# Pattern sums moved to GpSimd and merge weights spread by ScalarE and transposed, in the second layer's new-token attention

## The chip, the cores and the metric
One Trainium2 chip, one NeuronCore of it. The metric is the device time of one launch in microseconds, median of three runs.

## The reference, cut to what matters
The kernel runs one inference step of a two-layer decoder for a prompt of 1024 tokens and for 8 sample sequences of 8 new tokens each. Layer 2 attends with three head groups of different window and dilation over shared keys and values; the group outputs are merged with weights that are their softmax denominators, normalised over the groups.

```python
B_PATTERNS = ((128, 1), (512, 4), (2048, 16))       # (window, dilation), 8 heads of 64 each

def combine_groups(outs, lses):
    wts = jax.nn.softmax(jnp.stack(lses, axis=0), axis=0)
    return jnp.einsum('gnts,gntsd->ntsd', wts.astype(outs[0].dtype), jnp.stack(outs, axis=0))

def dilated_sample(q, kc, vc, slopes):
    S = q.shape[1]
    W = kc.shape[1] - S
    outs, lses = [], []
    for gi, (w, r) in enumerate(B_PATTERNS):
        steps = jnp.arange(w // r + 1)
        idx = W + jnp.arange(S)[:, None] - r * steps[None, :]
        valid = idx >= 0
        idx = jnp.maximum(idx, 0)
        kg = kc[:, idx]
        vg = vc[:, idx]
        s = jnp.einsum('bshd,bskhd->bhsk', q[:, :, gi], kg).astype(jnp.float32) * HEAD_DIM ** -0.5
        s = s - slopes[gi][None, :, None, None] * (r * steps).astype(jnp.float32)
        s = jnp.where(valid[None, None], s, NEG)
        lse = jax.nn.logsumexp(s, axis=-1)
        p = jnp.exp(s - lse[..., None])
        outs.append(jnp.einsum('bhsk,bskhd->bshd', p.astype(vc.dtype), vg))
        lses.append(jnp.swapaxes(lse, 1, 2))
    return combine_groups(outs, lses)
```

## The kernel before, in words
All activations stay in SBUF with features on partitions. The projections (L1447) are the bulk of the span: each weight block is split into a high and a low part, and three fp32r products are made of it. The order of the work is written out by hand: every engine has its own program, and they meet at semaphores that count completed steps.

The change touches one stage. After the attention of the second layer over the prompt (scores L1754, transposes of probabilities L1766, values L1783) come eight batches of new tokens, b = 0 to 7, one per sample sequence. They share one softmax over the three patterns, so the eight heads' rows of a batch hold 1344 columns of `PSB`: 512 for dilation 16, 512 for dilation 4, 128 for dilation 1, and 3 x 64 for the new tokens themselves. Per batch:

- `sample(b)` on GpSimd (L578) stages the queries into `SQN`, two buffers in turn.
- `sample_scores(b)` on TensorE (L1802 to L1811) makes the scores of all patterns; it waits until VectorE has read those of the batch before (`sb_ttr`).
- `sample(b)` on VectorE (L1333, L1339) adds the penalties in four pieces and keeps a running minimum, each piece waiting for the one before; `sample(b)` on ScalarE (L860) exponentiates all 1344 columns in place.
- `sample_turn(b)` on TensorE (L1835) transposes the probabilities by matmuls with the identity. A key that belongs to several patterns gets the sum of its probabilities: the matmuls of its segments accumulate into the same PSUM columns (14 matmuls).
- ScalarE (L868) and VectorE (L1357, L1358) copy the result to `PTS`; `sample_values(b)` on TensorE (L1860, L1862) multiplies with the values.
- ScalarE scales by the reciprocal sum (L875), TensorE transposes the output back (L1867), ScalarE and VectorE write its high and low parts (L882, L1365).

Between these steps stands the merge of the prompt's three pattern outputs, cut into 8 pieces (p, h), where `pieces(b)` gives batch 0 two of them, batches 1 to 6 one each, and batch 7 none. A piece has three rows, g = 0 to 2, numbered n = 3(2p + h) + g. `merge_row` on TensorE (L1823) spreads the weights `CW` of one pattern over 128 features into PSUM, with the weight column broadcast over 64 as the stationary operand and the identity moving (8 matmuls); `merge_product` on VectorE (L1314) multiplies the pattern's output with it; GpSimd (L587) adds the three. Every second batch, ScalarE and VectorE write the merged output's high and low parts (L886, and `merge_lo`, L1318).

TensorE's order in a batch is: scores of b + 1, turn of b, merge rows 0 and 1, values of b, merge row 2, output transpose of b, further rows. ScalarE's is: exponential of b + 1, copy to `PTS` of b, scaling of b, and the output parts. VectorE's: penalties of b + 1, copies to `PTS` of b, products, output parts. GpSimd's: staging of b + 2, adds. ScalarE and VectorE prepare the first weights of the output projection at the end of batch 6.

```python
            for b in range(NEWB):
                if b + 1 < NEWB:
                    sample(b + 1)
                sample_keys(b)
                sample_norm(b)
```

Of the kernel before, what the change touches and what calls it, by code (L numbers as in the profile page):

```python
# [20 lines left out]
P = 128  # L21
DM = 1024
SEQ = 1024
NEWB, NEWT = 8, 8
NEW = NEWB * NEWT
TOK = SEQ + NEW
KT = DM // P
HD = 64
# [3 lines left out]
NG = len(PATTERNS)  # L32
# [16 lines left out]
R16, R4, R1 = 512, 512, 128  # L49
# [43 lines left out]
def program(nc, t):  # L93
    from contextlib import ExitStack
    ctx = ExitStack()
    with ctx:
        base = [16512]

        def at(name, shape, off, dt=F32):
            return nc.alloc_sbuf_tensor_at(name, shape, dt, offset=off)  # L100

        def take(nbytes):
# [7 lines left out]
        o_xh, o_xl = take(KT * W4 + 256), take(KT * W4 + 256)  # L110
# [6 lines left out]
        IDN = at("IDN", [P, P], take(512))  # L117
# [54 lines left out]
        CM = at("CM", [P, 2, 8, 16], R + 71680)  # L172
        CW = at("CW", [P, NG, 8, 8], R + 72704)
        CS = at("CS", [P, NG, 8, 8], R + 73472)
        CT = [at("CT0", [P, 8, 8], R + 74240), at("CT1", [P, 8, 8], R + 74496)]
        TSB = at("TSB", [P, R16 + R4 + R1], R + 74752)

# [6 lines left out]
        PSB = at("PSB", [P, 2, SCOLS], o_xl + 16384)  # L184
        PTS = at("PTS", [P, 7, P], o_xl + 27136)
        PS = ctx.enter_context(nc.psum_tensor("PS", [P, 8, 512], F32))
# [1 line left out]
        names = """raw0 raw1 wh wl slab free0 free1 vps vev_act vev_dve const ones gain pad  # L188
            sq sqs sums std rb eps xh xn xfree silu gt yg yt yout tch tres tsq tadd tcol tstd trst trow scaled hh hx
            qev a_free a_score a_ttr a_exp a_rl a_norm a_tr a_pev0 a_pev1 a_pv a_out ohi olo xre  # L190
            score ttr exp tr pev0 pev1 pv oev stats cm0 cm1 c_d c_x c_op coef c_t c_mul c_add c_hi c_lo
            tabA nsink tab1 tab4 tab16 kperm vnew vst_out vg0 vg1
            cA tsa sa_q sa_s sa_ttr sa_exp sa_es sa_p sa_tr sa_evA sa_evD sa_pv sa_out sa_outlo
            home0 home1 home2 home3 home4 tsb sb_stage sb_zero sb_s sb_ttr sb_exp sb_p sb_tr sb_evA sb_evD sb_pv sb_os sb_otr sb_oh sb_ol
            ka0 ka1 khalf kwh kwl turn rows_out copies""".split()
        S = {n: ctx.enter_context(nc.semaphore("s_" + n)) for n in names}
        xin = [ctx.enter_context(nc.semaphore(f"s_xin{k}")) for k in range(KT)]
# [75 lines left out]
        def pieces(b):  # L273

            return (0, 1) if b == 0 else (b + 1,) if b + 1 < NEWB else ()
# [206 lines left out]
        def _(pool):  # L482
# [89 lines left out]
            def sample(b):  # L572
                if b >= 2:
                    pool.wait_ge(S["sb_s"], b - 1)
                for kk in range(2):
                    src = QB[64 * kk:64 * kk + 64, :].rearrange("p (a g n) -> p g a n", a=4, g=NG)[:, :, :, SEQ + b * NEWT:SEQ + (b + 1) * NEWT]
                    dst = SQN[b % 2][64 * kk:64 * kk + 64, :, :, 8 * kk:8 * kk + 8]
                    nc.gpsimd.tensor_copy(dst, src).then_inc(S["sb_stage"], 1)  # L578

            def add(p, h):  # L580

                n = 2 * p + h
                for g in (1, 2):
                    pool.wait_ge(S["c_mul"], 3 * n + g + 1)
                    if n or g == 2:
                        pool.wait_ge(S["c_add"], 2 * n + g - 1)
                    nc.gpsimd.tensor_tensor(as_tokens(natural(0, p, h).rearrange("p i r -> p (i r)"), g),  # L587
                                            as_tokens(natural(0, p, h).rearrange("p i r -> p (i r)"), g), natural(g, p, h),
                                            ALU.add).then_inc(S["c_add"], 1)
            sample(0)  # L590
            pool.wait_ge(S["sb_stage"], 2)
            pool.wait_ge(S["score"], C2)
            nc.gpsimd.memset(SQN[1][:], 0.0).then_inc(S["sb_zero"], 1)
            pool.wait_ge(S["sb_zero"], 2)
            sample(1)
            for b in range(NEWB):
                if b + 2 < NEWB:
                    sample(b + 2)
                pool.wait_ge(S["sb_stage"], 2 * min(b + 3, NEWB))
                for n in pieces(b):  # L600
                    add(n // 2, n % 2)
                    pool.wait_ge(S["c_add"], 2 * n + 2)
# [5 lines left out]
        def _(act):  # L608
# [237 lines left out]
            for s in range(C3 + T_LAG):  # L846
                n = len(CALLS[s]) if s < C3 else 0
# [15 lines left out]
            def sample_keys(b):  # L863

                act.wait_ge(S["sb_tr"], 2 * b + 1)
                if b:
                    act.wait_ge(S["sb_pv"], b)
                nc.scalar.copy(PTS[:, 0:4, :], PS[:, 5, :].rearrange("p (c n) -> p c n", c=4)).then_inc(S["sb_evA"], 1)  # L868

            def sample_norm(b):  # L870
                act.wait_ge(S["sb_pv"], b + 1)
                act.wait_ge(S["sb_p"], b + 1)
                if b:
                    act.wait_ge(S["sb_otr"], b)
                nc.scalar.activation(OS[:], PS[:, 7, 0:P], ACT.Copy, scale=SM[:, 8 + b % 2:9 + b % 2]).then_inc(S["sb_os"], 1)  # L875

            def sample_out(b):
                act.wait_ge(S["sb_otr"], b + 1)
                for kk in range(2):
                    src = PS[64 * kk:64 * kk + 64, 7, P:2 * P].rearrange("p (a n) -> p a n", a=4)[:, :, 8 * kk:8 * kk + 8]  # L880
                    dst = outputs(QBR, 1)[64 * kk:64 * kk + 64, :, SEQ + b * NEWT:SEQ + (b + 1) * NEWT]
                    nc.scalar.copy(dst, src).then_inc(S["sb_oh"], 1)  # L882

            def merge_hi(p):
                act.wait_ge(S["c_add"], 4 * p + 4)
                nc.scalar.copy(outputs(QBR, 1)[:, p, 0:SEQ], outputs(QB, 0)[:, p, 0:SEQ]).then_inc(S["c_hi"], 1)  # L886
            sample(0)
            act.wait_ge(S["c_d"], 2)
            nc.scalar.activation(CW[:], CW[:], ACT.Exp).then_inc(S["c_x"], 1)
            for b in range(NEWB):  # L890
                if b + 1 < NEWB:
                    sample(b + 1)
                sample_keys(b)
                sample_norm(b)
                if b % 2 == 1:
                    merge_hi(b // 2)
                sample_out(b)
                if b == NEWB - 2:
                    act.wait_ge(S["sb_pv"], NEWB - 1)
                    act.wait_ge(S["rows_out"], 80)  # L900
                    start("oB")
# [30 lines left out]
        def _(dve):  # L932
# [345 lines left out]
            def coefficients():  # L1278
# [15 lines left out]
                dve.wait_ge(S["c_x"], 1)  # L1294
                nc.vector.tensor_tensor(CS[:, 0], CW[:, 0], ST[:, 0, :, 8:16], ALU.mult)
                for x in range(2):
                    ins = nc.vector.tensor_tensor(CS[:, 1 + x], CW[:, 1 + x], CM[:, x, :, 8:16], ALU.mult)
                ins.then_inc(S["c_op"], 1)
# [3 lines left out]
                op(4)  # L1302
                nc.vector.reciprocal(CT[1][:], CT[0][:]).then_inc(S["c_op"], 1)
                op(5)
# [126 lines left out]
        def _(pe):  # L1431
            mm = nc.tensor.matmul
# [97 lines left out]
            for k in range(KT):  # L1530
# [17 lines left out]
                for j in range(2):  # L1548
                    ins = key_chunks(j, k, 2, WH, XL)
# [80 lines left out]
            for s in range(STEPS + PV_LAG_A):  # L1630
                dense, p = s < STEPS - 4, s - TR_LAG
# [66 lines left out]
            for j in range(2):  # L1698
                pe.wait_ge(S["wl"], PLAN.first["oA"] + j + 1)
                for k in range(KT):  # L1700
                    at = KT * j + k
# [11 lines left out]
            for j in range(2):  # L1713
                for k in range(KT):
                    ins = dense_o(j, k, (2,))
# [97 lines left out]

            def merge_row(p, h, g):

                pe.wait_ge(S["coef"], 1)
                n = 3 * (2 * p + h) + g
                if n >= 2:
                    pe.wait_ge(S["c_mul"], n - 1)
                for x in range(4):  # L1820
                    for kk in range(2):
                        c = CW[:, g, 4 * h + x, 2 * p + kk:2 * p + kk + 1].to_broadcast([P, HD])
                        ins = mm(PS[64 * kk:64 * kk + 64, 2 * (n % 2), x * P:(x + 1) * P], c, IDN[:], start=True, stop=True)  # L1823
                ins.then_inc(S["c_t"], 1)

            def sample_turn(b):
                j = b % 2
                pe.wait_ge(S["sb_exp"], b + 1)
                if b:
                    pe.wait_ge(S["sb_evA"], b)  # L1830
                    pe.wait_ge(S["sb_evD"], 2 * b)

                def turned(out, segs):
                    for n, (o, q0, w) in enumerate(segs):
                        ins = mm(out[o:o + w], PSB[:, j, q0:q0 + w], IDN[:], start=(n == 0), stop=(n == len(segs) - 1))  # L1835
                    return ins
                r4, r1, new = R16, R16 + R4, R16 + R4 + R1
                turned(PS[:, 5, 0:P], ((0, 0, P),))
                turned(PS[:, 5, P:2 * P], ((0, P, P),))
                turned(PS[:, 5, 2 * P:3 * P], ((0, 2 * P, P), (0, r4, P)))  # L1840
                turned(PS[:, 5, 3 * P:4 * P], ((0, 3 * P, P), (64, r1, 64), (0, r4 + P, P))).then_inc(S["sb_tr"], 1)
                turned(PS[:, 6, 0:P], ((0, r4 + 2 * P, P),))
                turned(PS[:, 6, P:2 * P], ((0, r4 + 3 * P, 64),))
                turned(PS[:, 6, P:2 * P], ((64, r4 + 3 * P + 64, 64), (64, r1 + 64, 64)))
                turned(PS[:, 6, 2 * P:3 * P], [(0, new + g * NEW, NEW) for g in range(NG)]).then_inc(S["sb_tr"], 1)

            def sample_values(b):
                vc = VC[b]
# [23 lines left out]
            for b in range(NEWB):  # L1872
# [3 lines left out]
                n = pieces(b)  # L1876
# [194 lines left out]
```

## Time and profile before
| | |
|---|---|
| median of 3 runs | 2524.53 us (2524.42 to 2526.21) |
| profiled execution, its own time | 2525.31 us |
| its span | 2523.5 us |
| TensorE matmul busy | 2451.0 us, 97% |
| VectorE, ScalarE, GpSimd busy | 1006.4, 656.5, 358.0 us |
| mean granted TensorE clock | 0.992 |
| the eight batches | 1574 to 1662 us of the span |

### The profile page before, as it was taken

Reading aid. Unit: us, or ns where it says so; the run is one execution under the profiler, and the core shown is the slowest. Engines: PE = TensorE matmul, PEld = TensorE weight load, DVE = VectorE, ACT = ScalarE, POOL = GpSimd, SP = SyncE. Lnnn points to the kernel's source line nnn. Section 1 sums busy time; section 2 is a strip of 40 time slices with the busy share of each in tenths; the row PEclk is TensorE's granted clock in tenths of the full one; section 3 lists DMA queues with packets and bytes.
Section 4 is the critical chain, followed back from the end, with each engine's and each line's share of the span. In section 5 each row is a group of like instructions: output and inputs, shape, how many; then the busy total and the mean of one; then the engine's idle time right before and its main releaser. Section 6 shows DMA issues by size and latency. Waiting matters only on the chain. (4 is left out here: it accounts for less than half of the span.)

```text
span 2523.5 us, 41269 instructions
## 1 busy us (share of the span) xinstructions
PE 2451.0 (97%) x16803; PEld 2367.1 (94%) x16803; DVE 1006.4 (40%) x1899; ACT 656.5 (26%) x1243; POOL 358.0 (14%) x242
## 2 busy tenths in 40 slices
PE   8999899999999999999999998999999999999997
PEld 7888699999999999999999876789999999999997
DVE  6466536232322322336312377656322332232235
ACT  4345424211111111113110187233311110111123
POOL 2333201101100100101111110311101100101100
PEclk9999999999999999999999999999999999999999
DMA  4010214113111311311221234713113111312212
GB/s 176 21 53 21 86 51 139 42 37 115 47 35 48 116 32 51 110 35 54 71 77 48 76 100 138 259 41 117 44 41 114 42 41 50 108 37 68 94 35 86
DMA packets 64942, 186.70 MB, mean 74 GB/s; under 512 B 11288, under 2 KB 17816, under 8 KB 64056
## 3 DMA queue, kind: packets, MB, share of 16 engines
q1 hardware_dynamic: 63928, 180.46, 22.3%
q0 software_dynamic: 912, 4.85, 0.5%
q8 instruction: 68, 1.11, 0.2%
q14 instruction: 34, 0.28, 0.0%
HBM read 175.85 MB, written 44.70 MB: 87 GB/s over the span
## 5 line engine op out<-in xcount | busy, mean ns | idle before, releaser
L935 DVE TENSOR_TENSOR WL<-RAW,WH 128x1024 fp32r<-128x1024 f32 (+3 forms) x196 | 219.4, 1120 | 1140.2 <-ACT WH L618 1139.6
L1447 PE MATMUL PS<-XH,WH 128*128 128x384 f32 x2640 | 582.6, 328 | 2.4 <-DVE XL L962 1.2
L1447 PE MATMUL PS<-XL,WH 128*128 128x384 f32 x2640 | 581.7, 328 | 0.0
L1447 PE MATMUL PS<-XH,WL 128*128 128x384 f32 x2640 | 581.7, 328 | 0.0
L618 ACT CAST WH<-RAW 128x1024 fp32r<-128x1024 f32 (+3 forms) x196 | 184.7, 944 | 1157.4 <-PE PS L1447 1142.7
L1447 PEld LDWEIGHTS PS<-XH,WH 128*128 128x128 f32 x2640 | 450.8, 188 | 3.5 <-DVE XL L962 1.5
L1447 PEld LDWEIGHTS PS<-XH,WL 128*128 128x128 f32 x2640 | 450.9, 188 | 0.0
L1447 PEld LDWEIGHTS PS<-XL,WH 128*128 128x128 f32 x2640 | 450.8, 188 | 0.0
L498 POOL TENSOR_TENSOR RAW<-RAW,GAIN 128x1024 f32<-128x1024 f32 x112 | 216.9, 1938 | 1641.1 <-DMA RAW<-in_w_gu 1386.7
L1447 PE MATMUL PS<-HH,WL 128*128 128x384 f32 (+1 forms) x1041 | 228.7, 327 | 0.0
L1447 PE MATMUL PS<-HL,WH 128*128 128x384 f32 (+1 forms) x1041 | 228.5, 327 | 0.0
L1447 PE MATMUL PS<-HH,WH 128*128 128x384 f32 (+1 forms) x1041 | 228.5, 327 | 0.0
L1447 PEld LDWEIGHTS PS<-HH,WH 128*128 128x128 f32 x1041 | 176.0, 188 | 0.0
L1447 PEld LDWEIGHTS PS<-HL,WH 128*128 128x128 f32 x1041 | 176.0, 188 | 0.0
L1447 PEld LDWEIGHTS PS<-HH,WL 128*128 128x128 f32 x1041 | 175.9, 188 | 0.0
L1145 DVE TENSOR_TENSOR XT<-XT,PS 128x768 f32 (+3 forms) x158 | 106.3, 714 | 3.5 <-PE PS L1447 3.4
L537 POOL TENSOR_TENSOR SA<-SA,SM 128x512 f32<-128x512 f32 (+1 forms) x64 | 72.3, 1132 | 129.3 <-DVE SM L1061 129.3
L711 ACT ACTIVATE SA<-SA,SM 128x257 f32<-128x257 f32 (+1 forms) x128 | 62.5, 491 | 98.5 <-DVE SM L1052 98.5
L836 ACT ACTIVATE SB<-SB,ST 128x128 f32<-128x128 f32 (+1 forms) x192 | 84.3, 446 | 8.7 <-DVE ST L1244 8.7
L1199 DVE TENSOR_TENSOR HL<-HT,HH 128x1088 f32 (+1 forms) x44 | 56.9, 1293 | 59.0 <-ACT HH L807 59.0
L807 ACT CAST HH<-HT 128x1088 f32 (+1 forms) x44 | 48.6, 1104 | 113.0 <-DVE HT L1196 113.0
L1191 DVE TENSOR_TENSOR GT<-GT,RB 128x1088 f32<-128x1088 f32 x44 | 56.9, 1293 | 52.0 <-ACT GT L803 52.0
(225 smaller groups left out, 2459.8 us busy)
## 6 DMA issues: line engine op xcount, KB each, us to landing
RAW<-in_w_gu SPq DMA_DIRECT2D x88, 512.0 KB, 3.6
out_bkS<-in_bk_in SPq DMA_DIRECT2D x8, 2032.0 KB
out_bvS<-in_bv_in SPq DMA_DIRECT2D x8, 2032.0 KB
RAW<-in_w_dn SPq DMA_DIRECT2D x32, 384.0 KB, 3.0
KC<-in_bk_in SPq DMA_DIRECT2D x8, 1536.0 KB, 7.8
VC<-in_bv_in SPq DMA_DIRECT2D x8, 1536.0 KB, 11.2
RAW<-in_w_dn SPq DMA_DIRECT2D x32, 320.0 KB, 2.8
XT<-in_xT SPq DMA_DIRECT2D x16, 544.0 KB, 5.5
```

What stands on the lines that cost most here:

```text
L498: nc.gpsimd.tensor_tensor(w, w, g, ALU.mult).then_inc(S["scaled"], 1)
L537: nc.gpsimd.tensor_tensor(p, p, SM[:, 24 + 2 * b:26 + 2 * b].unsqueeze(2).to_broadcast([P, 2, w]), ALU.mult).then_inc(S["a_norm"], 1)
L618: nc.scalar.copy(to[:, j, 0:nk * P], RAW[:, j, 0:nk * P]).then_inc(S["wh"], 1)
L711: ins = nc.scalar.activation(SA[:, b, kk, 256 - w:257], SA[:, b, kk, 256 - w:257], ACT.Exp, bias=SM[:, h:h + 1], scale=-1.0, accum_out=SM[ ...
L807: nc.scalar.copy(HH[:, ds(i * TOK, TOK)], HT[:]).then_inc(S["hh"], 1)
L836: ins = nc.scalar.activation(s, s, ACT.Exp, bias=ST[:, g, blk, 2 * p + kk:2 * p + kk + 1], scale=-1.0, accum_out=ST[:, g, blk, 8 + 2 * p + ...
L935: nc.vector.tensor_tensor(lo[:, j, 0:nk * P], RAW[:, j, 0:nk * P], hi[:, j, 0:nk * P].bitcast(F32), ALU.subtract).then_inc(S["wl"], 1)
L1145: ins = nc.vector.tensor_tensor(x, x, ps, ALU.add)
L1191: nc.vector.tensor_tensor(GT[:], GT[:], RB[:], ALU.mult).then_inc(S["gt"], 1)
L1199: nc.vector.tensor_tensor(HL[:, ds(i * TOK, TOK)], HT[:], HH[:, ds(i * TOK, TOK)].bitcast(F32), ALU.subtract).then_inc(S["hx"], 1)
L1447: ins = mm(PS[:, 3 * j + c, 0:width], w[:, j, k * P:(k + 1) * P], x(k, a, width), start=(k == 0 and n == 0), stop=(k == nk - 1 and n == 2))
```

## The change
GpSimd adds up the columns of keys that belong to several patterns, in five adds per batch inside `PSB`, after the exponential; the turn is then seven plain transposes, without accumulation. ScalarE spreads each row of merge weights to a 128x512 tile `CB` (two buffers of it in turn), and TensorE transposes that in four transposes instead of eight matmuls with a broadcast operand. TensorE's turn waits for the last add (`sb_add`) instead of the exponential, and a merge row for ScalarE's copy (`c_b`). The order of the batches, and of the other steps in them, is as before.

```diff
+        CB = at("CB", [P, 2, 512], o_xh + 28672)
...
+            def pattern_sums(b):
+
+                x = PSB[:, b % 2, :]
+                pool.wait_ge(S["sb_exp"], b + 1)
+                nc.gpsimd.tensor_tensor(x[:, 256:512], x[:, 256:512], x[:, R16:R16 + 256], ALU.add).then_inc(S["sb_add"], 1)
+                new = R16 + R4 + R1
+                nc.gpsimd.tensor_tensor(x[:, new:new + NEW], x[:, new:new + NEW], x[:, new + NEW:new + 2 * NEW], ALU.add).then_inc(S["sb_add"], 1)
+                pool.wait_ge(S["sb_add"], 5 * b + 1)
+                nc.gpsimd.tensor_tensor(x[:, 448:512], x[:, 448:512], x[:, R16 + R4:R16 + R4 + 64], ALU.add).then_inc(S["sb_add"], 1)
+                nc.gpsimd.tensor_tensor(x[:, 960:1024], x[:, 960:1024], x[:, R16 + R4 + 64:R16 + R4 + R1], ALU.add).then_inc(S["sb_add"], 1)
+                pool.wait_ge(S["sb_add"], 5 * b + 2)
+                nc.gpsimd.tensor_tensor(x[:, new:new + NEW], x[:, new:new + NEW], x[:, new + 2 * NEW:new + 3 * NEW], ALU.add).then_inc(S["sb_add"], 1)
...
+            pool.wait_ge(S["sb_stage"], 4)
+            pattern_sums(0)
+            pool.wait_ge(S["sb_add"], 5)
             for b in range(NEWB):
                 if b + 2 < NEWB:
                     sample(b + 2)
                 pool.wait_ge(S["sb_stage"], 2 * min(b + 3, NEWB))
+                if b + 1 < NEWB:
+                    pattern_sums(b + 1)
+                    pool.wait_ge(S["sb_add"], 5 * b + 10)
                 for n in pieces(b):
...
+            def merge_spread(p, h, g):
+                n = 3 * (2 * p + h) + g
+                act.wait_ge(S["coef"], 1)
+                if n >= 2:
+                    act.wait_ge(S["c_t"], n - 1)
+                c = CW[:, g, 4 * h:4 * h + 4, 2 * p:2 * p + 2].unsqueeze(3).to_broadcast([P, 4, 2, HD])
+                nc.scalar.copy(CB[:, n % 2, :].rearrange("p (b k d) -> p b k d", b=4, k=2), c).then_inc(S["c_b"], 1)
...
             for b in range(NEWB):
+                n = pieces(b)
+                if n:
+                    merge_spread(n[0] // 2, n[0] % 2, 0)
+                    merge_spread(n[0] // 2, n[0] % 2, 1)
                 if b + 1 < NEWB:
                     sample(b + 1)
                 sample_keys(b)
+                if n:
+                    merge_spread(n[0] // 2, n[0] % 2, 2)
                 sample_norm(b)
                 if b % 2 == 1:
                     merge_hi(b // 2)
                 sample_out(b)
+                for x in n[1:]:
+                    for g in range(NG):
+                        merge_spread(x // 2, x % 2, g)
...
             def merge_row(p, h, g):
 
-                pe.wait_ge(S["coef"], 1)
                 n = 3 * (2 * p + h) + g
+                pe.wait_ge(S["c_b"], n + 1)
                 if n >= 2:
                     pe.wait_ge(S["c_mul"], n - 1)
                 for x in range(4):
-                    for kk in range(2):
-                        c = CW[:, g, 4 * h + x, 2 * p + kk:2 * p + kk + 1].to_broadcast([P, HD])
-                        ins = mm(PS[64 * kk:64 * kk + 64, 2 * (n % 2), x * P:(x + 1) * P], c, IDN[:], start=True, stop=True)
+                    ins = nc.tensor.transpose(PS[:, 2 * (n % 2), x * P:(x + 1) * P], CB[:, n % 2, x * P:(x + 1) * P], IDN[:])
                 ins.then_inc(S["c_t"], 1)
 
             def sample_turn(b):
                 j = b % 2
-                pe.wait_ge(S["sb_exp"], b + 1)
+                pe.wait_ge(S["sb_add"], 5 * b + 5)
...
-                turned(PS[:, 5, 0:P], ((0, 0, P),))
-                turned(PS[:, 5, P:2 * P], ((0, P, P),))
-                turned(PS[:, 5, 2 * P:3 * P], ((0, 2 * P, P), (0, r4, P)))
-                turned(PS[:, 5, 3 * P:4 * P], ((0, 3 * P, P), (64, r1, 64), (0, r4 + P, P))).then_inc(S["sb_tr"], 1)
-                turned(PS[:, 6, 0:P], ((0, r4 + 2 * P, P),))
-                turned(PS[:, 6, P:2 * P], ((0, r4 + 3 * P, 64),))
-                turned(PS[:, 6, P:2 * P], ((64, r4 + 3 * P + 64, 64), (64, r1 + 64, 64)))
-                turned(PS[:, 6, 2 * P:3 * P], [(0, new + g * NEW, NEW) for g in range(NG)]).then_inc(S["sb_tr"], 1)
+                for c in range(4):
+                    ins = nc.tensor.transpose(PS[:, 5, c * P:(c + 1) * P], PSB[:, j, c * P:(c + 1) * P], IDN[:])
+                ins.then_inc(S["sb_tr"], 1)
+                for c in range(2):
+                    q = R16 + (2 + c) * P
+                    nc.tensor.transpose(PS[:, 6, c * P:(c + 1) * P], PSB[:, j, q:q + P], IDN[:])
+                new = R16 + R4 + R1
+                nc.tensor.transpose(PS[0:NEW, 6, 2 * P:3 * P], PSB[:, j, new:new + NEW], IDN[:]).then_inc(S["sb_tr"], 1)
```

TensorE, one batch from its turn to its output transpose, before (PSB: probabilities, CW: merge weights, IDN: identity, PTS: transposed probabilities, OS: scaled output):

```order
L1835 MATMUL PS<-IDN,PSB 128x128 x5
L1835 MATMUL PS<-IDN,PSB 64x128
L1835 MATMUL PS<-IDN,PSB 128x128 x2
L1835 MATMUL PS<-IDN,PSB 64x128 x6
L1823 MATMUL PS<-IDN,CW 64x128 x16
L1860 MATMUL PS<-VC_123,PTS 32x128 x24
L1862 MATMUL PS<-VNB,PTS 32x128 x4
L1823 MATMUL PS<-IDN,CW 64x128 x8
L1867 MATMUL PS<-IDN,OS 128x128
```

The same place with the change:

```order
L1867 MATMUL PS<-IDN,PSB 128x128 x4
L1871 MATMUL PS<-IDN,PSB 128x128 x2
L1873 MATMUL PS<-IDN,PSB 64x128
L1857 MATMUL PS<-IDN,CB 128x128 x8
L1888 MATMUL PS<-VC_124,PTS 32x128 x24
L1890 MATMUL PS<-VNB,PTS 32x128 x4
L1857 MATMUL PS<-IDN,CB 128x128 x4
L1895 MATMUL PS<-IDN,OS 128x128
```

The places in the order are the same; 14 matmuls became 7 transposes, and each row's 8 became 4 transposes.

ScalarE, one batch with `merge_hi`, before:

```order
L860 ACTIVATE PSB,SM<-PSB,SM 128x1344
L868 COPY PTS<-PS 128x512
L875 ACTIVATE OS<-PS,SM 128x128
L886 CAST QBR<-QB 128x1024
L882 CAST QBR<-PS 64x4x8 x2
```

And with the change:

```order
L909 COPY CB<-CW 128x512 x2
L879 ACTIVATE PSB,SM<-PSB,SM 128x1344
L887 COPY PTS<-PS 128x512
L909 COPY CB<-CW 128x512
L894 ACTIVATE OS<-PS,SM 128x128
L913 CAST QBR<-QB 128x1024
L901 CAST QBR<-PS 64x4x8 x2
```

Two copies stand ahead of the exponential of the next batch, the third between the copy to `PTS` and the scaling.

## Rows read from the trace of the kernel before
**Rows 1.** The page's first part: busy time, share and instructions of each engine.
```profile
PE 2451.0 (97%) x16803; PEld 2367.1 (94%) x16803; DVE 1006.4 (40%) x1899; ACT 656.5 (26%) x1243; POOL 358.0 (14%) x242
```
**Rows 2.** Chain of waits, 1560 to 1670 us: start, us, what.
```profile
1615.76 0.59 ACT PTS L868
1616.39 1.52 PE PS L1860 x48
...
1619.34 1.16 DVE QB L1314
...
1620.84 1.24 DVE QBR L1318
1622.08 1.16 issue
```
**Rows 3.** Timeline, batch 3: start, us, engine, line, operation [idle before, releaser].
```profile
1611.07 3.29 PE L1835 MATMUL PS<-IDN,PSB 128*128 128x128 f32 x27
...
1611.38 0.69 DVE L1333 CUSTOM_DVE_ANT_0 PSB<-PS,TSB 128x512 f32<-128x512 f32 x1 [1.44 <-PE PS L1811]
...
1614.09 0.32 PE L1823 MATMUL PS<-IDN,CW 128*64 128x128 f32 x1
...
1614.22 1.42 ACT L860 ACTIVATE PSB<-PSB,SM 128x1344 f32<-128x1344 f32 x1 [5.08 <-DVE SM L1339]
...
1618.19 1.09 PE L1823 MATMUL PS<-IDN,CW 128*64 128x128 f32 x16
1618.33 0.37 ACT L875 ACTIVATE OS<-PS,SM 128x128 f32<-128x128 f32 x1 [1.99 <-PE PS L1862]
...
1619.22 0.33 PE L1867 MATMUL PS<-IDN,OS 128*128 128x128 f32 x1
...
1619.48 1.06 PE L1802 MATMUL PS<-KC,SQN 128*32 128x512 f32 x8
```
**Rows 4.** The same timeline: first add, the next scores' end, the next two V.
```profile
1617.51 1.52 POOL L587 TENSOR_TENSOR QB<-QB 128x512 f32<-128x512 f32 x1 [5.59 <-issue]
...
1621.44 0.52 PE L1811 MATMUL PS<-KNB,SQN 128*32 128x64 f32 x24
...
1628.25 1.52 PE L1860 MATMUL PS<-VC,PTS 128*32 128x128 f32 x48 [1.21 <-ACT PTS L868]
...
1639.07 1.52 PE L1860 MATMUL PS<-VC,PTS 128*32 128x128 f32 x48 [0.18 <-ACT PTS L868]
```
**Rows 5.** Groups by form, 1574.7 to 1662 us: busy us, mean ns.
```profile
L1835 PE MATMUL PS<-IDN,PSB 128*128 128x128 f32 x112 | 16.6, 289 | 0.0
...
L1835 PE MATMUL PS<-IDN,PSB 128*64 128x128 f32 x112 | 12.2, 283 | 0.0
```
**Rows 6.** Attention-stage timeline; L1766's ns (minimum, median, maximum); groups by form.
```profile
1558.44 1.09 PE L1766 MATMUL PS<-IDN,SB 128*128 128x128 f32 x8
...
1560.26 1.09 PE L1783 MATMUL PS<-PT,VG 128*64 128x128 f32 x16 [0.72 <-DVE PT L1265]
...
L1766 PE MATMUL PS<-IDN,SB x280: 272/273/474, 1447.8 to 1562.1; 128*128 128x128 f32 x140
...
L868 ACT COPY PTS<-PS 128x512 f32<-128x512 f32 x8 | 4.7, 584 | 0.5 <-PE PS L1835 0.3
...
L537 POOL TENSOR_TENSOR SA<-SA,SM 128x256 f32<-128x256 f32 x8 | 5.1, 636 | 28.9 <-DVE SM L1061 28.9
```
**Rows 7.** Windows: us, busy (count) of PE, PEld, DVE, ACT, POOL; clock, DMA, GB/s.
```profile
1553.80:1561.00 7.20, 4.98 (x62) 4.25 (x64) 4.20 (x20) 5.65 (x26) 0.00 (x0) 1.00 0.06 7
...
1567.50:1570.60 3.10, 0.00 (x0) 0.01 (x1) 2.37 (x9) 0.10 (x1) 0.53 (x2) 1.00 1.05 402
1570.90:1574.30 3.40, 3.40 (x29) 1.36 (x25) 2.40 (x11) 1.36 (x3) 0.00 (x0) 0.50 1.03 408
...
1604.40:1605.50 1.10, 0.00 (x0) 0.00 (x0) 1.10 (x2) 1.08 (x3) 0.00 (x0) 1.00 1.01 371
...
1239.80:1242.20 2.40, 0.01 (x2) 0.01 (x1) 1.28 (x2) 1.99 (x2) 0.00 (x0) 1.00 0.00 0
1243.30:1246.50 3.20, 3.20 (x17) 3.20 (x17) 1.30 (x3) 0.00 (x0) 0.44 (x1) 0.50 0.80 205
```

More of the change, by code:

```diff
@@ L190, in program @@
             qev a_free a_score a_ttr a_exp a_rl a_norm a_tr a_pev0 a_pev1 a_pv a_out ohi olo xre
-            score ttr exp tr pev0 pev1 pv oev stats cm0 cm1 c_d c_x c_op coef c_t c_mul c_add c_hi c_lo
+            score ttr exp tr pev0 pev1 pv oev stats cm0 cm1 c_d c_x c_op coef c_b c_t c_mul c_add c_hi c_lo
             tabA nsink tab1 tab4 tab16 kperm vnew vst_out vg0 vg1
             cA tsa sa_q sa_s sa_ttr sa_exp sa_es sa_p sa_tr sa_evA sa_evD sa_pv sa_out sa_outlo
-            home0 home1 home2 home3 home4 tsb sb_stage sb_zero sb_s sb_ttr sb_exp sb_p sb_tr sb_evA sb_evD sb_pv sb_os sb_otr sb_oh sb_ol
+            home0 home1 home2 home3 home4 tsb sb_stage sb_zero sb_s sb_ttr sb_exp sb_add sb_p sb_tr sb_evA sb_evD sb_pv sb_os sb_otr sb_oh sb_ol
             ka0 ka1 khalf kwh kwl turn rows_out copies""".split()
@@ L1831, in sample_turn @@
                     pe.wait_ge(S["sb_evD"], 2 * b)
[L1833 to L1837, printed above, removed]
-                turned(PS[:, 5, 0:P], ((0, 0, P),))
-                turned(PS[:, 5, P:2 * P], ((0, P, P),))
-                turned(PS[:, 5, 2 * P:3 * P], ((0, 2 * P, P), (0, r4, P)))
-                turned(PS[:, 5, 3 * P:4 * P], ((0, 3 * P, P), (64, r1, 64), (0, r4 + P, P))).then_inc(S["sb_tr"], 1)
-                turned(PS[:, 6, 0:P], ((0, r4 + 2 * P, P),))
-                turned(PS[:, 6, P:2 * P], ((0, r4 + 3 * P, 64),))
-                turned(PS[:, 6, P:2 * P], ((64, r4 + 3 * P + 64, 64), (64, r1 + 64, 64)))
-                turned(PS[:, 6, 2 * P:3 * P], [(0, new + g * NEW, NEW) for g in range(NG)]).then_inc(S["sb_tr"], 1)
+                for c in range(4):
[6 more added lines that the diff above has]
+                nc.tensor.transpose(PS[0:NEW, 6, 2 * P:3 * P], PSB[:, j, new:new + NEW], IDN[:]).then_inc(S["sb_tr"], 1)
             def sample_values(b):
```

## The prediction, made before the changed kernel was run
> **What bounds the kernel now.** The page's first part shows TensorE busy for 97% of the span [rows 1], and the windows of the stage that the diff touches (the eight batches of new tokens, from about 1574 to 1662 us) show it nearly as full. Busy time suggests that every matmul saved is time saved. I read the chain of waits next, because it tells which piece ended each wait. One batch goes from one run of `sample_values` (L1860, called V here) to the next. V starts at 1616.39, 1628.25 and 1639.07 us [rows 2, 4]: 11.86 us for a batch with a `merge_lo` and 10.82 us for one without, 22.68 us for the pair. The reader is to see that the piece in front of V is not a matmul but ScalarE's copy L868 [rows 2].
>
> The timeline of the same batch says what that copy stands behind [rows 3]. The scores of the next batch release VectorE's masking chain at 1611.38 (L1333 and L1339), that releases the exponential L860 at 1614.22, and only then does ScalarE, in its own order, copy the transposed patterns and let V go at 1616.39: 5.01 us without TensorE. Meanwhile TensorE does `sample_turn` (1611.07) and two merge rows (from 1614.09), which end 0.18 us before V. They fill a wait that exists without them. So TensorE looks full, yet the loop is scores, VectorE, ScalarE, V, and back.
>
> **The change part by part.** *sample_turn* issued 14 matmuls per batch, 3.02 us from its start at 1611.07 to the merge row at 1614.09 [rows 3]; over the stage its two forms have 16.6 and 12.2 us [rows 5]. Seven transposes take their place. The same operation on the same shape stands in the attention stage: eight in 1.09 us, the last of them 0.27 us long, so (1.09 - 0.27) / 7 = 0.117 us each [rows 6]. Seven make 0.82 us, 2.2 us less per batch, 17.6 us over eight.
>
> *merge_row* issued 8 matmuls, 1.03 us a row (1618.19 to 1619.22) [rows 3]; four transposes take 0.47 us, 0.56 us less, and 24 rows make 13.4 us. Together TensorE loses about 31 us of work. Of that the part ahead of V (2.2 + 2 x 0.56 = 3.3 us a batch) lies wholly in the wait above, and is worth nothing there: V still comes 5.01 us after the scores let VectorE go.
>
> *The third merge row* stands after V. Today the output transpose L1867 starts at V + 2.83 because the row ahead of it ends then. With a row of 0.47 us TensorE is free at V + 1.80 + 0.47 = V + 2.27, but its input comes from the scaling L875, which ran from V + 1.94 to V + 2.31 [rows 3]. So the output transpose starts at about V + 2.36 and the next scores 0.26 us later, 0.47 us earlier than now. In a batch with `merge_lo` the way is another one: the product L1314 of that row (1619.34), then L1318, which shows 1.16 us of waiting while GpSimd's add L587 runs, then L1333 at 1623.24, where the scores had ended by 1621.96 [rows 2, 4]. The product waits for the row, starts 4 transposes after V + 1.80, at V + 1.80 + 3 x 0.117 + 0.27 + 0.06 = V + 2.48 instead of V + 2.95: again 0.47 us. The collision of L1318 with the add stays, since both follow the same product. Seven steps from V to V make 7 x 0.47 = 3.3 us. At the end the last turn gets 2.2 us shorter, but VectorE's splitting of the first output weights holds the copies behind it; I give it 0.3 us. **Saved: 3.6 us.**
>
> *GpSimd's pattern sums*: five adds a batch. Width 256 has a row, 0.64 us [rows 6]; the four of 64 columns have none: between 0.16 (a quarter of it) and 0.64 us each. I take 0.25, nearer the narrow end because the width is a quarter, and 0.1 for each of three waits: 1.9 us, at most 3.5. They start when the exponential of the next batch ends (V - 0.7) and the turn that needs them starts at V + 5.0. Cover: 5.7 us. Behind them in GpSimd's order stands the first add of the merge, which started at V + 1.12 [rows 4] and now finds the sums done at about V - 0.7 + 1.9 = V + 1.2, so it is put off by 0.1 us, 1.7 at the worst, and is long over when the second is due at V + 3.7. Cost: nothing, bounds 0 and 0.5 us a batch (the second add late by that much). The sample copies follow in the same order and are needed 8 us later.
>
> *ScalarE's copies into CB*: 24 of 128x512. The nearest row is the copy L868, 0.58 us [rows 6]; a source with stride 0 has no row, so from 0.5 to 1.0 us, and I take 0.6. Two stand ahead of the exponential, on which ScalarE now waits 5.08 us [rows 3]; the third stands between L868 and L875, where 1.99 us are free. Cost: nothing. If either copy took over 1.3 us, the scaling L875 would be late by the excess. In the first batch the three extra rows wait for copies and products in turn (about 0.6 and 0.7 us each), which gives about the same 0.4 us.
>
> **The clock** is what the saved work costs. With turn and rows gone, TensorE has nothing from V + 5.03 + 0.82 + 0.94 = V + 6.8 to the next V at V + 10.35 or V + 11.4: stalls of 3.5 and 4.6 us, where it is 0.18 and 1.21 us now. The windows show what such stalls do [rows 7]: after 3.1 us without a matmul (from 1567.5) and after 2.4 us (from 1239.8) the granted clock went to 0.50, the 1.2 GHz level, and stayed so for 3.4 us; through the 1.1 us at 1604.4 it stayed at 1.00, 2.4 GHz. 3.4 us at half speed is 1.7 us lost. What runs behind each new stall (V, the output transpose, the next scores) is on the path. Eight stalls (batches 0 to 7) could cost 0 to 13.6 us. Some will miss a fall, and part of a slow stretch may lie in the stall or in the hidden row, so I take three quarters, 1.3 us: **+10.4 us**.
>
> The attention windows from 1553.8 held 1.00 [rows 7], though their matmuls were eight transposes in 1.09 us for every sixteen value records in 1.09 us [rows 6]. That is why I count only true stalls as idle. The Trainium skill, page "TensorE: Matmul & The Clock Gate", section "Part 4: PE-mode transpose", says that transposes do not count as activity for the clock. By that rule turn and rows would be idle time too, the falls surer and longer, which is rival C below; this trace speaks against it.
>
> Sum: -3.6 + 10.4 = +6.8 us on the profiled execution's 2525.3 us, 2532.1 us. The median of the runs is 0.8 us lower, so 2531.3 us. A measurement of this kernel can tell about 0.2%, 5 us, from no change.
>
> **The rivals.**
> A, *the clock stays at 2.4 GHz* through the stalls: only the saving is left, -3.6 us, 2520.9 us, with -7 if the add and L1318 also stop colliding (three times 1.16 us). For it: the stalls are regular and short and the stretches between them dense. Against: both stalls of over 2.3 us above were answered by a fall. It decides if a stall of 3.5 us leaves the clock at 1.00. This is the case on the other side, not slower.
> B, *TensorE's time is the time*: 31 us gone, 2493.5 us. For it: 97% busy. Against: the chain, where V waits for ScalarE, with 1.21 us of TensorE idle already in every second batch.
> C, *the clock stays low longer*, through turn and rows into the next V. All of V, the output step and the scores (1.80 + 0.26 + 2.41 us) at half speed would be 4.5 us in each of seven batches, +31 - 3.6, 2552 us at worst; half of that, 2538 us, is likelier. The quoted rule about transposes would lead here. Against it: 1.00 in the attention windows, and a return after 3.4 us in the two other cases.
> D, *the pattern sums are late*: decides above 5.7 us for the five adds plus the 3.5 us of stall, over 9 us a batch. Each excess microsecond costs 8. Even five adds at 1.0 us stay under it.
>
> **How the numbers follow.** Forecast 0.60, A 0.22, B 0.03, C 0.12, D 0.03. The forecast's own range is +2 to +11 us. The range given goes from A's 2520 to 2537 us, just short of C's likelier value, which leaves out B, half of C and the tails. Slower by over 5 us: three quarters of the forecast's 0.60, all of C, most of D, 0.58. Faster by over 5 us: B and A's far end, 0.08. Within: 0.34.
>
> **What would show it.** In the changed profile V should still start about 5.0 us after L1333's first piece when the clock is full; TensorE should show 3 to 5 us of idle before every V, released by ScalarE's copy; the granted clock should have some five to eight more stretches at 0.50 between 1574 and 1665 us, each starting near V. TensorE's busy time should fall by much less than 31 us since some of it runs at half speed. The sums should end over 3 us ahead of the turn. I am wrong if the stage is shorter by more than 7 us (the chain is misread), if the clock stays at 1.00, or if the turn waits for GpSimd.

## The result, and the profile after
The changed kernel takes 2535.54 us (median of 7 runs, 2532.60 to 2537.26), the kernel before 2525.86 us (7 runs, 2524.42 to 2528.15): a ratio of 1.0042, 95% interval 1.0033 to 1.0051, or 9.7 us slower. The profiled execution took 2535.54 us with a span of 2533.8 us, 10.3 us more than that of before.

The page's first part of the changed kernel, and the clock line of its second. Engines' busy us and share, then the clock in 40 slices:

```profile
PE 2430.7 (96%) x16347; PEld 2347.6 (93%) x16347; DVE 1006.0 (40%) x1899; ACT 669.6 (26%) x1267; POOL 373.6 (15%) x282
...
PEclk9999999999999999999999999889999999999999
```

TensorE is busy for 20.3 us less than in [rows 1], though 31 us of work were counted away: the work that is left in the same stage now runs at half speed for a good part. The two slices with an 8 are that stage, the eight batches of new tokens.

Timeline of batches 1 and 2 (start, us, engine, line, operation, and in brackets the idle time before and what ended it). L1888 are the values (V), L1857 the merge rows, L894 the scaling, L1895 the output transpose, L1838 to L1847 the next scores, L1867 the turn, L1369 and L1375 the penalties, L879 the exponential:

```profile
1595.89 1.52 PE L1888 MATMUL PS<-VC,PTS 128*32 128x128 f32 x48 [3.48 <-ACT PTS L887]
...
1597.69 0.66 PE L1857 MATMUL PS<-IDN,CB 128*128 128x128 f32 x4
...
1597.83 0.37 ACT L894 ACTIVATE OS<-PS,SM 128x128 f32<-128x128 f32 x1 [1.47 <-PE PS L1890]
...
1598.25 0.33 PE L1895 MATMUL PS<-IDN,OS 128*128 128x128 f32 x1
...
1598.51 1.06 PE L1838 MATMUL PS<-KC,SQN 128*32 128x512 f32 x8
...
1600.91 0.66 PE L1867 MATMUL PS<-IDN,PSB 128*128 128x128 f32 x4
...
1601.73 1.04 PE L1857 MATMUL PS<-IDN,CB 128*128 128x128 f32 x8
1602.30 0.69 DVE L1369 CUSTOM_DVE_ANT_0 PSB<-PS,TSB 128x512 f32<-128x512 f32 x1
...
1605.14 1.41 ACT L879 ACTIVATE PSB<-PSB,SM 128x1344 f32<-128x1344 f32 x1 [4.56 <-DVE SM L1375]
...
1607.31 2.55 PE L1888 MATMUL PS<-VC,PTS 128*32 128x128 f32 x48 [4.54 <-ACT PTS L887]
```

This step ran at full clock up to its end, and it is the one that answers to [rows 2 to 4]. V comes 5.01 us after L1369, as it did before. The output transpose starts at V + 2.36 instead of V + 2.83, the whole step is 11.42 us instead of 11.86, and the 2.2 us of turn and the 1.1 us of rows that are gone have become idle time: 3.48 us before the first V, 4.54 us before the second, where the same two steps had 0.19 and 1.21 us before. Turn and rows end at 1602.77, long ahead of the copy L887 that lets V go. The second V is the same work as the first and takes 2.55 instead of 1.52 us.

The windows of the same stage say why (us, then busy time and count of PE, PEld, DVE, ACT and POOL, the granted clock, DMA share, GB/s):

```profile
1580.30:1583.70 3.40, 2.71 (x48) 2.12 (x48) 0.75 (x1) 1.15 (x4) 3.01 (x6) 0.50 0.02 7
1607.70:1611.00 3.30, 3.30 (x55) 2.53 (x44) 0.00 (x0) 0.44 (x2) 2.45 (x5) 0.50 0.04 11
1617.90:1624.60 6.70, 5.50 (x69) 3.61 (x73) 2.17 (x4) 3.66 (x9) 3.36 (x6) 0.50 0.55 162
1631.60:1638.30 6.70, 5.87 (x69) 3.70 (x73) 2.12 (x4) 2.79 (x9) 3.59 (x7) 0.50 0.34 86
1645.20:1648.50 3.30, 3.12 (x56) 2.37 (x56) 0.10 (x1) 0.64 (x2) 3.03 (x6) 0.50 0.64 245
1658.90:1662.20 3.30, 3.30 (x48) 2.53 (x38) 0.00 (x0) 0.37 (x1) 2.23 (x4) 0.50 0.02 5
1665.70:1675.80 10.10, 7.07 (x68) 6.00 (x69) 2.72 (x7) 1.56 (x4) 0.00 (x0) 0.50 0.16 52
...
1592.50:1595.80 3.30, 0.00 (x0) 0.00 (x0) 2.92 (x11) 2.06 (x4) 0.43 (x1) 1.00 0.49 181
```

Each of the first seven lies on or right behind a V that had waited; four of them begin 0.7 to 1.2 us ahead of it, in the stall. They are at 0.50, the 1.2 GHz level, for 37 us together; the kernel before had none from 1574.3 us to 1662.68, where the output projection starts, and one of 3.4 us right behind. The last line is the stall ahead of V at 1595.89: nothing on TensorE for 3.3 us, and the clock stayed at 1.00. Seven of eight stalls were answered by a fall.

From the first V to the first weights of the output projection the stage takes 91.6 us (1580.99 to 1672.57) against 82.8 us (1579.88 to 1662.68). Of the span's 10.3 us that is 8.8; 1.1 us had been lost before the first V, and 0.4 behind. The 1.1 us are older than the changed work: the first scores of the new tokens already start at 1566.14 instead of 1564.98 us.

### The profile page after: what moved, and what is told of

It reads as the page before. It is cut to its first block and busy times, and to the rows that moved or that the text cites. A ratio compares the mean times of both kernels' runs of the same rounds, so it can differ in the third digit from the quotient of the medians.

```text
span 2533.8 us, 40451 instructions
## 1 busy us (share of the span) xinstructions
PE 2430.7 (96%) x16347; PEld 2347.6 (93%) x16347; DVE 1006.0 (40%) x1899; ACT 669.6 (26%) x1267; POOL 373.6 (15%) x282
```

## The experiments
Two questions stood: is it the clock, or the new work of ScalarE and GpSimd; and which half of the change does it. All seven kernels were timed beside the kernel before, whose medians there were 2524.01 us (32 runs, first four kernels) and 2524.39 us (18 runs, last three). V's lines below are from the timeline of each kernel's profiled execution.

### The changed kernel with transposes in its stalls
```diff
                     merge_row(n[0] // 2, n[0] % 2, 1)
+                if b:
+                    pe.wait_ge(S["sb_ol"], 2 * b)
+                for _ in range(26):
+                    nc.tensor.transpose(PS[:, 7, 384:512], IDN[:], IDN[:])
                 sample_values(b)
```

> As fill_mm, but the filler is 26 transposes of the identity (2.8 to 3.0 us). If transposes keep the clock up as matmuls do: the same time as fill_mm within 1.5 us and a granted clock of 1.00. If they do not count as activity: the clock falls as in the changed kernel, and the time is near 2535 us.

And the same with matmuls:

```diff
+                for _ in range(11):
+                    mm(PS[:, 7, 384:512], IDN[:], IDN[:], start=True, stop=True)
```

> The changed kernel with 11 matmuls of the identity by the identity (2.4 to 3.0 us, their results are not used) in each stall ahead of the values, so that TensorE has work there while the path is the same. Clock theory: the granted clock stays at 1.00 through the eight batches, and only the saving is left: 3 to 4 us below the kernel before, about 13 us below the changed kernel. Rival 'the time is lost in ScalarE's or GpSimd's new work': as slow as the changed kernel or slower, about 2535 us.

Measured: 2523.08 us with transposes (11 runs, ratio to before 0.9996, interval 0.9987 to 1.0004), 2525.14 us with matmuls (11 runs, 0.9999, 0.9990 to 1.0007). Both do all that the changed kernel does and more, and are 10 to 12 us faster than it. With the transposes (L1867 is the turn, L1911 the filler, L1857 the merge rows):

```profile
1579.93 1.52 PE L1888 MATMUL PS<-VC,PTS 128*32 128x128 f32 x48
...
1583.74 1.18 PE L1857 MATMUL PS<-IDN,CB 128*128 128x128 f32 x8 [1.12 <-ACT CB L909]
...
1588.23 0.66 PE L1867 MATMUL PS<-IDN,PSB 128*128 128x128 f32 x4
...
1589.93 3.00 PE L1911 MATMUL PS<-IDN 128*128 128x128 f32 x26
...
1593.57 1.52 PE L1888 MATMUL PS<-VC,PTS 128*32 128x128 f32 x48 [0.64 <-ACT PTS L887]
...
1605.04 1.52 PE L1888 MATMUL PS<-VC,PTS 128*32 128x128 f32 x48 [1.74 <-ACT PTS L887]
...
1615.39 1.52 PE L1888 MATMUL PS<-VC,PTS 128*32 128x128 f32 x48 [0.63 <-ACT PTS L887]
...
1626.83 1.52 PE L1888 MATMUL PS<-VC,PTS 128*32 128x128 f32 x48 [1.72 <-ACT PTS L887]
...
1655.77 1.52 PE L1888 MATMUL PS<-VC,PTS 128*32 128x128 f32 x48
...
1579.90:1660.00 80.10, 68.88 (x1064) 53.59 (x1064) 50.39 (x114) 35.64 (x71) 41.69 (x61) 1.00 0.61 212
```

The steps are 11.47, 10.35 and 11.44 us (forecast 11.39 and 10.35), every V takes 1.52 us, and the clock is 1.00 over the stage (last line, its window). First V to output projection is 80.03 us here (1579.93 to 1659.96) and 91.58 us in the changed kernel, so the falls that the stalls bring cost 11.5 us in these two profiles. The new work of ScalarE and GpSimd is in both, so it can't be what makes the difference. That settles the first question.

The matmul filler missed its forecast of a clock at 1.00 and 3 to 4 us below the kernel before; its median is 1.1 us above. It was shorter than meant and left 1.0 and 2.1 us of stall, and in the profiled execution, the slowest of its eleven (2531.13 us), two of the three stalls of 2.1 us in the stage were still followed by a fall (V of 2.70 and 2.05 us). It shows the same direction with less force. The two fillers lie 2.1 us apart, where 1.5 were expected.

### Half of the change each
Only the merge rows (against the changed kernel: `sample_turn` as before, no sums):

```diff
-            pattern_sums(0)
-            pool.wait_ge(S["sb_add"], 5)
...
-                if b + 1 < NEWB:
-                    pattern_sums(b + 1)
-                    pool.wait_ge(S["sb_add"], 5 * b + 10)
```

> Only the merge rows are changed (copies of ScalarE and four transposes); the turn and the sums stay as in the kernel before. Clock theory: TensorE has 2.2 us more work in front of each run of values than in the full change, so the stalls shrink from about 3.5 and 4.6 us to 1.4 and 2.4 us; the clock falls once to three times more than before instead of at nearly every batch; the saving of 0.47 us per batch, 3.3 us in all, stays. Time 2 to 4 us below the kernel before, 2521.5 to 2524 us. Rival 'the copies or the transposes themselves are slow': the time is above the kernel before, as with the full change. Rival 'TensorE's time is the time': 13 us below.

Only the turn (`merge_row` as before, no `merge_spread`):

```diff
-                    merge_spread(n[0] // 2, n[0] % 2, 0)
-                    merge_spread(n[0] // 2, n[0] % 2, 1)
...
-                    merge_spread(n[0] // 2, n[0] % 2, 2)
...
-                        merge_spread(x // 2, x % 2, g)
```

> Only the turn is changed (GpSimd's pattern sums, seven transposes); the merge rows stay as in the kernel before. Clock theory: stalls of about 2.4 and 3.5 us before the values and nothing saved on the path, since the row behind the values is long again; four to seven stretches at 0.50; 4 to 8 us above the kernel before, about as slow as the full change. Rival 'no clock effect': equal to the kernel before within 1 us. Rival 'the sums on GpSimd are late': the turn waits for GpSimd in every batch, and the time is above the kernel before although the granted clock is no lower.

Measured: rows only 2522.82 us (11 runs, 0.9996, interval 0.9987 to 1.0004), turn only 2530.86 us (9 runs, 1.0024, 1.0014 to 1.0034). Rows only, three V:

```profile
1602.31 1.52 PE L1888 MATMUL PS<-VC,PTS 128*32 128x128 f32 x48 [1.96 <-ACT PTS L881]
...
1612.66 1.52 PE L1888 MATMUL PS<-VC,PTS 128*32 128x128 f32 x48 [0.90 <-ACT PTS L881]
...
1624.09 1.52 PE L1888 MATMUL PS<-VC,PTS 128*32 128x128 f32 x48 [1.97 <-ACT PTS L881]
```

Turn only, three V:

```profile
1594.03 1.52 PE L1881 MATMUL PS<-VC,PTS 128*32 128x128 f32 x48 [2.46 <-ACT PTS L887]
...
1605.89 2.55 PE L1881 MATMUL PS<-VC,PTS 128*32 128x128 f32 x48 [3.48 <-ACT PTS L887]
...
1618.26 1.52 PE L1881 MATMUL PS<-VC,PTS 128*32 128x128 f32 x48 [2.44 <-ACT PTS L887]
```

The rows alone carry the whole gain on the path: steps of 10.35 and 11.43 us, as with the full change at full clock, and stalls of 0.9 and 2.0 us with one fall in the stage, behind a stall of 1.97 us. The turn alone gains nothing on the path: 1594.03 to 1605.89 is 11.86 us, to the hundredth the step of before. It only lengthens the stalls, to 2.4 and 3.5 us, and the V behind both stalls of 3.48 us run slow (2.55 and 2.79 us). Its median is 6.9 us above the kernel before, as forecast (4 to 8). So the half that takes most work off TensorE (17.6 of 31 us) is the one that costs time. For rows only, the forecast was 2 to 4 us below the kernel before; the medians differ by 1.2 us, and the interval holds both no gain and 3 us.

### More work on GpSimd
```diff
-                pool.wait_ge(S["sb_add"], 5 * b + 2)
+                pool.wait_ge(S["sb_add"], 5 * b + 4)
+                for o, w in ((R16, 256), (R16 + R4, 128), (new + NEW, NEW)):
+                    nc.gpsimd.tensor_tensor(x[:, o:o + w], x[:, o:o + w], x[:, o:o + w], ALU.add)
```

> The changed kernel with three more GpSimd adds per batch (256, 128 and 64 columns of values no longer needed, about 1.6 us) in front of the last counted one. Clock theory: the sums have over 5 us of cover; the turn never waits for GpSimd after the first batch, and the time is that of the changed kernel within 2 us (2533 to 2538 us; the first batch can be 1.5 us later). Rival 'GpSimd's sums are on the path': 8 x 1.6 = 13 us above the changed kernel.

Measured: 2530.84 us (7 runs, 1.0026, interval 1.0013 to 1.0039). The sums now take 3.1 us instead of 1.8. The waits between 1570 and 1668 us name the turn behind GpSimd once, in the first batch (us in total, times, longest):

```profile
PE PS L1869 <- POOL PSB L604: 2.2, 1, 2.2
```

Were the sums on the path, this kernel would be some 10 us slower than the changed one. It is not slower at all; the median is 4.7 us lower, below the 2533 to 2538 us that were expected, and the two intervals just overlap. I read nothing into that difference: in its profile the stage has a mean clock of 0.84 against 0.82, and which stalls are followed by falls is not the same in every run. The sums' cover, 5.7 us by the forecast, is there: 3.1 us of sums fit into it.

### Another order, with and without the change
If V waits only because ScalarE and VectorE serve the next batch first, then serving batch b first should pay, and the change should be what makes it possible, since the turn must be short for that.

ScalarE, VectorE and TensorE, in this order:

```diff
-                if b + 1 < NEWB:
-                    sample(b + 1)
                 sample_keys(b)
                 if n:
                     merge_spread(n[0] // 2, n[0] % 2, 2)
                 sample_norm(b)
+                sample_out(b)
+                if b + 1 < NEWB:
+                    sample(b + 1)
                 if b % 2 == 1:
                     merge_hi(b // 2)
-                sample_out(b)
...
+                sample_keys(b)
+                sums(b)
                 if b + 1 < NEWB:
                     sample(b + 1)
                 else:
                     start("oB")
-                sample_keys(b)
-                sums(b)
...
                 sample_values(b)
+                sample_out(b)
                 if n:
                     merge_row(n[0] // 2, n[0] % 2, 2)
-                sample_out(b)
```

> The changed kernel with the order of the batches changed on three engines: ScalarE copies to PTS, scales and writes the output of batch b before the exponential of b + 1; VectorE copies to PTS before the penalties of b + 1; TensorE's output transpose stands before the third merge row. If the chain is what I read (V waits for the exponential of the next batch, though its own turn is long done), the step from V to V falls from 10.4 and 11.4 us to 8 to 9 us, the stalls get shorter than 2 us, and the time is 12 to 20 us below the kernel before, 2504 to 2512 us. Rival: VectorE (penalties 2.7, copies 0.6, products 2.8, outputs 0.4, every second batch 1.2 to 2.4 us more) becomes the bound with waits on GpSimd's sums, step about 10 us: 3 to 7 us below the kernel before. If ScalarE's copy was not the wait: no faster than the changed kernel.

> The same change of order made in the kernel before, with the turn and the merge rows as matmuls. TensorE's own work per batch (scores 2.4, turn 3.0, rows 3.1, values 1.8, output 0.3: 10.6 us) is then the bound, so the step stays near 10.7 us: 0 to 5 us below the kernel before. If that and reorder come out alike, the saved TensorE work is worth nothing in the new order either.

Measured: with the change 2511.45 us (5 runs, ratio 0.9947, interval 0.9934 to 0.9960), 13 us below the kernel before; the same order in the kernel before 2525.47 us (11 runs, 1.0005, 0.9996 to 1.0014), no difference. This is the version that beats both kernels, and its time is in the range expected for it; for the same order without the change 0 to 5 us below the kernel before were expected, and it is 1.1 us above. The reordered kernel's V, and its busy time over the stage:

```profile
1596.72 1.52 PE L1888 MATMUL PS<-VC,PTS 128*32 128x128 f32 x48
...
1605.20 1.52 PE L1888 MATMUL PS<-VC,PTS 128*32 128x128 f32 x48
...
1614.74 1.52 PE L1888 MATMUL PS<-VC,PTS 128*32 128x128 f32 x48
...
1575.80:1647.00 71.20, 51.91 (x882) 35.38 (x881) 48.98 (x122) 36.99 (x73) 43.46 (x61) 0.95 0.69 245
```

The steps are 8.48 and 9.54 us, and the stage is 71.3 us long instead of 82.8. In the kernel before, the same order gives steps of 11.13 us (V at 1602.22 and 1613.35), TensorE's own work of about 10.6 us and a wait of 0.49 us for the scaling. So the change costs 10 us in the old order and is worth 14 us in this one (2525.47 to 2511.45 us). In the step that ends at 1614.74, one with `merge_lo`, TensorE's longest wait is the one for GpSimd's sums:

```profile
1610.68 0.32 POOL L597 TENSOR_TENSOR PSB<-PSB 128x64 f32<-128x64 f32 x1
...
1610.95 1.23 DVE L1354 TENSOR_TENSOR QBR<-QB,QBR 128x1024 fp32r<-128x1024 f32 x1
1610.96 1.39 POOL L599 TENSOR_TENSOR PSB<-PSB 128x64 f32<-128x64 f32 x1
...
1612.96 0.66 PE L1867 MATMUL PS<-IDN,PSB 128*128 128x128 f32 x4 [1.23 <-POOL PSB L602]
```

In the step before, without `merge_lo`, that wait is 0.29 us, beside 0.68 us for VectorE's products and 0.49 us for the scaling; what holds up the sums in the other is told at the end. The expected waits of under 2 us held but for one of 2.35 us, the sums' in the last batch, in which the clock fell; the expected step of 8 to 9 us held for the batches without `merge_lo`.

## Why the prediction was right, and where its sizes were off
**The bound.** Right, and shown: V waits for ScalarE's copy, 5.01 us after the scores let VectorE go, in both kernels; the turn alone moved no step, and the new order took 1.9 us off each step of the change at full clock (10.35 to 8.48 and 11.43 to 9.54 us) without a faster instruction.

**The saving.** The mechanism and the size per step are right: steps of 11.42 and 10.35 us at full clock (forecast 11.39 and 10.35). The sum of 3.6 us was too high. From first to last V the kernel with transposes in its stalls takes 75.84 us against 78.61 us: 2.8 us. The first step gave 0.2 us instead of 0.47, the five behind it 0.39 to 0.46, the last one 0.43; the 0.3 us added for the end did not come, since from the last V to the output projection both kernels take 4.19 us.

**Prices of new instructions.** The copies to CB took 617 ns (0.6 taken); the sums 727 ns for 256 columns and 318 ns for 64 (0.64 and 0.25 taken), 1.8 us with their waits (1.9 summed); the turn's four large transposes 0.50 us (1600.91 to 1601.41) and all seven 0.82 us, from 1600.91 to the next row at 1601.73. From the second batch on none is on the path. In the first the copies are, which the forecast put at no loss: TensorE waits 1.12 us for them ahead of the extra rows (line of 1583.74 above), the next scores stand behind these rows, and this fits the 0.2 us instead of 0.47.

**The clock.** The step of the forecast that was mis-sized, and it carried the result. It was eight stalls at 1.3 us, 10.4 us, each fall 3.4 us long. There were seven falls after eight stalls, but three of them lasted 6.8, 6.8 and 10.2 us, and together they cost 11.5 us. Forecast: -3.6 + 10.4 = +6.8 us. In the stage the profiles show -2.8 + 11.5 = +8.8 us, rounded. The medians have +9.7 us. The extra 1.1 us that the profiled span lost ahead of the stage is no work of the change. That the clock term came close is luck in part. Eight falls of 3.4 us are 27 us at half speed, which can lose 13.6 us, of which the forecast took three quarters. The stretches came to 37 us, which can lose 18, but only 11.5 us of that lay on the path: longer stretches and a smaller share nearly made up for each other.

**The rivals.** A, a clock that stays up, is refuted by the windows. Its price can be read from the kernel with the filler of transposes: -2.8 us in the stage, and a median 0.9 us below the kernel before with an interval down to 3.3 us, where -3.6 us was forecast. B, TensorE's time is the time, is refuted by every run. D is refuted by the longer sums. C is right in that three stretches lasted longer than 3.4 us, so that V, the output step and part of the scores ran slow; but none lasted through turn and rows into the next V. The stretches around 1620 and 1635 us end in the scores (1624.7 and 1638.3), and the turn at 1626.54 is at full clock. The filler of transposes, with turn and rows being transposes too, held the clock at 1.00 for the 80 us of the stage, also from the turn at 1588.23 to V at 1593.57, 5.34 us in which TensorE had nothing but transposes and 0.64 us of idle time. The Trainium skill, page "TensorE: Matmul & The Clock Gate", section "Part 4: PE-mode transpose", says that transposes do not count as activity for the clock; for these fp32 transposes the measurement says that they do, and it decides.

**Left open.** Why the clock held through the stall of 3.48 us ahead of V at 1595.89 and fell after stalls of the same length ahead of 1619.10 and 1645.38 isn't settled; no run was made for it. Ahead of a V, stalls of 0.6 to 1.7 us had no fall behind them in the stage of the kernel with transposes, stalls of 3.5 us and more nearly always had. In between both occur: of ten stalls of 2.0 to 2.5 us in rows only, turn only and the kernel with the matmul filler, four were followed by a fall.

## What to carry to other kernels
When an engine looks full, find out whether its work lies ahead of a wait that exists anyway; taking such work away buys idle time, and behind idle time of 2 to 4.5 us what came next on TensorE often ran at half speed here. Change the order that makes the wait together with the work in it: here each alone gave nothing or a loss, and both together 13 us. If the order can't be changed, keep only the half of an edit that shortens the path, or leave TensorE something to do in the stall.

## What the runs showed of the hardware that was not expected
Stretches at half clock lasted 3.4, 6.8 or 10.2 us. The forecast knew only 3.4 us from [rows 7], and priced each fall by that, though the trace of the kernel before has a stretch of 6.8 us as well: from 1448.1 to 1454.8 us the granted clock is 0.50.

These transposes kept the clock up: 26 of them in each stall, and 1.00 throughout.

In the reordered kernel a GpSimd add of 64 columns took 1.39 us while VectorE ran L1354, which has two inputs in SBUF, and 0.32 us otherwise, which is about the difference between the steps of 9.54 and 8.48 us; in the kernel before it is L1318, the same operation, that waits for GpSimd's add [rows 2] and takes 2.37 instead of 1.23 us. Whichever gets in first holds the other up until it is done. The Trainium skill, page "SBUF — State Buffer", section "Who interferes with whom", states this rule, and the trace agrees, with 1.07 us lost by the second in this case.
